# One more stage of lead for the attention scores of a Hymba-style encoder layer, and the ratio of the two softmax sums formed by GpSimd

## The reference, cut to what matters

```python
s = jnp.einsum('bqhcd,bkhcd->bhcqk', qblk, kf) + bias[None, :, None]
pr = jax.nn.softmax(s, axis=-1)
w = pr[:, :, 0] - lam * pr[:, :, 1]
return jnp.einsum('bhqk,bkhe->bqhe', w, vf)
```

## Time and profile before

| | |
|---|---|
| time of the kernel before, median of 3 runs | 1044.28 us (1043.69 to 1045.43) |
| the profiled execution's own time | 1045.79 us |
| its span in the trace | 1044.0 us |
| PE, PEld busy | 1008.5 us (97%), 800.3 us (77%) |
| DVE, ACT, POOL busy | 659.5 (63%), 580.8 (56%), 500.5 us (48%) |
| mean granted TensorE clock | 0.994 of full speed |

### The profile page before, as it was taken

How to read it: one execution, slowest core, us unless ns; L and a number is a source line. 1 busy time by engine, 2 the same in 40 slices (tenths; PEclk the granted TensorE clock), 3 DMA queues, 4 the chain that set the end, 5 groups by cost and what they waited for, 6 DMA issues and landing times.

```text
span 1044.0 us, 15464 instructions
## 1 busy us (share of the span) xinstructions
PE 1008.5 (97%) x5792; PEld 800.3 (77%) x5792; DVE 659.5 (63%) x1055; ACT 580.8 (56%) x890; POOL 500.5 (48%) x404
## 2 busy tenths in 40 slices
PE   8999999999999999989999999999999999999997
PEld 6877777767787888857777777777788888888886
DVE  4654958583493250259999999999966244445423
ACT  7738485744641131269999999999952221122112
POOL 1233245526566550036667767766667244354421
PEclk9999999999999999999999999999999999999999
DMA  9651543323255526839687478363285222432221
GB/s 337 241 169 36 172 147 101 116 81 115 77 162 164 159 81 188 243 101 243 167 197 210 110 192 223 82 159 122 68 300 167 86 87 86 137 121 86 100 87 41
DMA packets 105929, 150.34 MB, mean 144 GB/s; under 512 B 10232, under 2 KB 68728, under 8 KB 105848
## 3 DMA queue, kind: packets, MB, share of 16 engines
q1 hardware_dynamic: 105712, 149.36, 47.5%
q10 hardware_dynamic: 144, 0.00, 0.0%
HBM read 102.07 MB, written 44.11 MB: 140 GB/s over the span
## 4 chain that ended last, share of the span: by engine, by line
PE 63%; DVE 19%; issue 10%; ACT 3%; POOL 2%; DMA 2%; SPq 0%; DVEq 0%; POOLq 0%; ACTq 0%
DVE E_ L1638 11%; PE b_ps L1917 5%; PE b_ps L1919 5%; PE b_ps L1918 5%; PE b_ps L1814 4%; PE g_ps L1816 4%; PE g_ps L1814 4%; PE g_ps L1815 4%; PE b_ps L1815 4%; PE b_ps L1816 4%; PE o_ps L1980 3%; PE w_ps L1963 2%; PE h_ps L1814 2%; PE h_ps L1816 2%; PE h_ps L1815 2%
## 5 line engine op out<-in xcount | busy, mean ns | idle before, releaser
L1251 ACT ACTIVATE E_<-E_,nmax 128x1024 f32<-128x1024 f32 (+1 forms) x184 | 186.7, 1018 | 15.0 <-DVE nmax L1638 14.8
L1638 DVE CUSTOM_DVE_ANT_0 E_<-s_ps,bias 128x1024 f32<-128x1024 f32 (+1 forms) x184 | 188.0, 1056 | 3.6 <-PE s_ps L1930 3.6
L969 POOL TENSOR_TENSOR E_<-E_,ratio 128x576 f32<-128x576 f32 (+3 forms) x92 | 84.5, 919 | 85.8 <-DVE E_ L1654 85.8
L1816 PE MATMUL b_ps<-u_hi,wA_lo 128*128 128x512 f32 x288 | 113.3, 394 | 0.0
L972 POOL TENSOR_TENSOR E_<-E_ 128x576 f32<-128x576 f32 (+3 forms) x92 | 103.7, 1127 | 7.2
L1930 PE MATMUL s_ps<-KL,QL 128*128 128x512 f32 x256 | 90.7, 435 | 13.9 <-DVE nmax L1638 13.1
L1814 PE MATMUL b_ps<-u_hi,wA_hi 128*128 128x512 f32 x240 | 96.7, 403 | 5.0 <-DVE u_lo L1410 2.8
L1815 PE MATMUL b_ps<-u_lo,wA_hi 128*128 128x512 f32 x240 | 94.7, 395 | 0.0
L1963 PE MATMUL w_ps<-ident,E_ 128*128 128x128 f32 x624 | 83.4, 273 | 1.8 <-ACT WT L1282 1.7
L1282 ACT ACTIVATE WT<-w_ps 128x1024 f32<-128x1024 f32 (+1 forms) x96 | 83.3, 868 | 2.8 <-PE w_ps L1963 2.6
L1980 PE MATMUL o_ps<-WT,V 128*64 128x128 f32 x1280 | 84.0, 278 | 0.0
(11 more groups left out here) (228 smaller groups left out, 2329.6 us busy)
## 6 DMA issues: line engine op xcount, KB each, us to landing
QL<-qk_t SPq DMA_DIRECT2D x32, 256.0 KB, 6.9
KL<-qk_t SPq DMA_DIRECT2D x32, 256.0 KB, 8.2
bias<-line_d SPq DMA_DIRECT2D x8, 960.0 KB, 11.8
x_sb<-in_x SPq DMA_DIRECT2D x12, 512.0 KB, 9.0
z_ch<-z_stage SPq DMA_DIRECT2D x24, 256.0 KB, 2.7
qk_t<-qh SPq DMA_DIRECT2D x24, 256.0 KB, 2.3
qk_t<-ql SPq DMA_DIRECT2D x24, 256.0 KB, 2.8
mf<-mix_t SPq DMA_DIRECT2D x24, 256.0 KB, 3.8
```

The costliest lines, as they stand in the source:

```text
L1251: act.activation(e, e, ACT.Exp, bias=nmax[:, n % 5, c:c + 1], scale=-1.0, accum_out=sums[:, n % 5, c:c + 1]).then_inc(e_done, 1)
L1638: dve.tensor_tensor_reduce(weights_at(n)[:, c, 0:n_tok], s_ps[:, c, 0:n_tok], b[:, ::-1], -1.0, 3e38, ALU.add, ALU.min, nmax[:, n % 5, c:c ...
L1816: mm = pe.matmul(dst, sl, mh, start=False, stop=k == n - 1)
```

## The change

The lead of `scores` and `biased` grows from four steps to five (RING), that of `exps` from three to four, that of `combine` from two to three. Seven steps (EARLY), four short and three long ones, have their scores between the V tiles 4 to 10. A long step's second map needs PSUM bank 3, which was a V tile's, so that the V tiles 3, 6 and 9 go to `qT_ps` (`v_bank`); `E_SLOT` only says which slot of the ring a step has. DVE's order in an iteration is now `factor`, `biased(., 0)`, `combine`, `biased(., 1)`. `ratio` is no longer formed on DVE but by `share(n)` on GpSimd, which stands ahead of GpSimd's `combine(n)`. SP's program is the same.

```diff
+        EARLY, RING = 7, 5
+        def steps_to(n, done, lead):
+            return min(NSTEP, max(min(done + n + 1, EARLY + 2), n + 1 + lead)) if n >= 0 else done
+        def due(n, done, lead):
+            return range(steps_to(n - 1, done, lead), steps_to(n, done, lead))
...
+            def share(n):
+                gp.wait_ge(r_done, n + 1)
+                if n >= 4:
+                    gp.wait_ge(w_dve, n - 3)
+                    gp.wait_ge(scaled, n - 3)
+                gp.tensor_scalar(ratio[:, n % 4:n % 4 + 1], sums[:, n % 5, 0:1], rsum[:, n % 24, 1:2], neglam[:],
+                                 ALU.mult, ALU.mult).then_inc(rr_done, 1)
...
             for n in range(NSTEP):
                 blk, head, u, qt = STEPS[n]
+                share(n)
                 combine(n)
...
             def factor(n):
                 dve.wait_ge(e_done, 2 * n + 2)
                 dve.reciprocal(rsum[:, n % 24, :], sums[:, n % 5, :]).then_inc(r_done, 1)
-                dve.wait_ge(r_done, n + 1)
-                if n >= 4:
-                    dve.wait_ge(w_gp, n - 3)
-                dve.scalar_tensor_tensor(out=ratio[:, n % 4:n % 4 + 1], in0=sums[:, n % 5, 0:1],
-                                         scalar=rsum[:, n % 24, 1:2], in1=neglam[:], op0=ALU.mult, op1=ALU.mult
-                                         ).then_inc(rr_done, 1)
...
-                if n + 2 < NSTEP:
-                    factor(n + 2)
-                    combine(n + 2)
-                if n + 4 < NSTEP:
-                    biased(n + 4, 0)
-                    biased(n + 4, 1)
+                for m in due(n, EARLY - 2, RING - 2):
+                    factor(m)
+                for m in due(n, EARLY, RING):
+                    biased(m, 0)
+                for m in due(n, EARLY - 2, RING - 2):
+                    combine(m)
+                for m in due(n, EARLY, RING):
+                    biased(m, 1)
...
-                if 2 * NT + 7 <= n < 2 * NT + 11:
+                if 3 * NT - EARLY - 1 <= n < 3 * NT - 1:
...
-                if n + 4 < NSTEP:
-                    scores(n + 4, 0)
+                for m in due(n, EARLY, RING):
+                    scores(m, 0)
                 turn(n)
-                if n + 4 < NSTEP:
-                    scores(n + 4, 1)
+                for m in due(n, EARLY, RING):
+                    scores(m, 1)
```

More of the change, by code:

```diff
@@ L238, in encoder_layer @@
         phase2.close()
+        E_SLOT = (3, 1, 0, 4, 2)
         def weights_at(n):
-            return Es[:, n, :, :] if n < 4 else E[:, n % 5, :, :]
+            return Es[:, n, :, :] if n < 4 else E[:, E_SLOT[n % 5], :, :]
         def q_tile(u, hh):
@@ L366, in split_at, with v_bank @@
             return {(1, 1): 448, (1, 0): 768, (0, 0): 256, (0, 1): 128}[(int(long_now), int(long_next))]
+        EARLY, RING = 7, 5
[3 more added lines that the diff above has]
+            return range(steps_to(n - 1, done, lead), steps_to(n, done, lead))
+        def v_bank(t):
+            return b_ps[:, t % NB, :] if t % NB or not t else qT_ps[:, 0, :, :].rearrange("p a b -> p (a b)")
         def fill_count(n):
@@ L1264, in _ @@
                     act.wait_ge(x_rs, 3 * NB)
-                act.activation(sq_junk[:, t % 2, :], b_ps[:, t % 3, :], ACT.Copy, scale=rsx[:, t:t + 1]
+                act.activation(sq_junk[:, t % 2, :], v_bank(t), ACT.Copy, scale=rsx[:, t:t + 1]
                                ).then_inc(v_evac, 1)
@@ L1269, in _ @@
                     wl_high(2 * t - 13)
-                if t >= 9:
+                if t >= NT - EARLY:
                     for c in range(2):
-                        exps(t - 9, c)
+                        exps(t - NT + EARLY, c)
             def weights_out(n):
@@ L1305, in _ @@
                 blk, head, u, qt = STEPS[n]
-                if n + 3 < NSTEP:
-                    exps(n + 3, 0)
+                for m in due(n, EARLY, RING - 1):
+                    exps(m, 0)
                 if qt == 1 and blk:
                     heads_out(blk - 1)
-                if n + 3 < NSTEP:
-                    exps(n + 3, 1)
+                for m in due(n, EARLY, RING - 1):
+                    exps(m, 1)
                 if half_out_at(n):
@@ L1673, in wl_low @@
                                   ).then_inc(wl_lo_done, 1)
-            for n in range(4):
+            for n in range(EARLY):
                 for c in range(2):
                     biased(n, c)
-                if n < 2:
-                    wl_low(2 * n)
-                    wl_low(2 * n + 1)
+                if n in (3, 4):
+                    wl_low(2 * n - 6)
+                    wl_low(2 * n - 5)
                 if n >= 2:
@@ L1914, in qkv_tile @@
                     pe.wait_ge(v_evac, 2 + n - 2 * NT - NB + 1)
-                dst = b_ps[:, n % NB, :]
+                if g == 2 and t == NB:
+                    pe.wait_ge(qlo_done, 2 * NT - 1)
+                dst = v_bank(t) if g == 2 else b_ps[:, n % NB, :]
                 for k in range(KC):
@@ L1935, in _ @@
                 qkv_tile(n)
-                if 2 * NT + 7 <= n < 2 * NT + 11:
-                    if n == 2 * NT + 7:
+                if 3 * NT - EARLY - 1 <= n < 3 * NT - 1:
+                    if n == 3 * NT - EARLY - 1:
                         pe.wait_ge(sig_done, UNITS_C * LC)
                     for c in range(2):
-                        scores(n - 2 * NT - 7, c)
+                        scores(n - 3 * NT + EARLY + 1, c)
                 if n == 2:
```

## The result

| | before | after |
|---|---|---|
| median | 1044.69 us (1043.69 to 1045.43, 4 runs) | **1087.2 us** (1084.65 to 1087.94, 4 runs) |
| profiled execution, span | 1044.0 us | 1082.9 us |
| granted clock | 0.994 | 0.989 |
| DVE, ACT, POOL busy | 63%, 56%, 48% | 59%, 54%, 49% |

The ratio is 1.0403, 95% interval 1.0384 to 1.0423: 4% slower. The direction was forecast; the time is 24 us over the forecast's 1063 and outside its range.

What follows compares the result with a forecast made beforehand. DVE was taken as the bound, ACT 5% behind, GpSimd with room. Loop +1.5, `wa_low` +19.2, ACT's lag +1.0, start -0.5 and end -2.6 gave +18.6 on 1045.8: 1064.4, or 1063 for the median; range 1049 to 1072.

Steps and rivals of the forecast that it cites:

- the two `combine`s alternate: Attention loop: DVE's and GpSimd's `combine` can't overlap; long rounds 3.74 us, a head 38.4 against 38.29; forecast case's chance 0.72.
- without its 79 us of waits for DVE: Sign expected in the profile after: GpSimd no longer shows its 79 us of waits for DVE.
- `wa_low` in the round: First two short steps of heads 2 to 5: `wa_low` delays the next `ratio`, 4.8 us a head, 19.2 us together.
- the forecast's wait for `wa_hi`: Sign expected at heads 2 to 5: behind its `wa_low`, GpSimd shows a wait for `wa_hi` of about 2.5 us.
- up to 0.7 at three heads, 0 to 2.1; I take 1: Three heads without `wa_high`: ACT's lag through `half_out` may cost up to 0.7 us each; counted as +1.0 us.
- the short rounds: Loop's short steps, two of each form a head: 2.85 us (768/256), 2.31 (256/256), 2.84 (128/384, DVE's own work).
- ACT's lag and the bias: Loop: ACT's lag through `half_out` counted at 1 us; `biased(12)` waiting for head 1's bias loads at 1.1 us.
- The start: Before the loop: loop starts at 461.3 instead of 458.13, `combine(9)` at 481.9 instead of 483.54, 1.6 us won.
- The end: Behind `combine(95)`: `turn(95)` comes about 3.4 us later instead of 6.0, with PE ahead: -2.6 us.
- The rule weighed: GpSimd contends with DVE instructions having two SBUF inputs, so its halves could shorten; the sum kept their lengths, following a 0.61 us row.

Runs made afterwards that it cites:

- the run with the ratio alone: Kernel before with only `ratio` moved to GpSimd, `share(n)` ahead of its `combine(n)`, leads as before: 1069.24 us (ratio 1.0241).
- lead-four run: Changed kernel with the loop's old leads (scores 4, `exps` 3, `combine` 2), seven early steps, new DVE order and ratio on GpSimd kept: 1067.87 us (1.0232).
- the two with the ratio between: `share(n + 1)` put between GpSimd's multiply and add, `share(0)` ahead of the loop: in the changed kernel 1068.9 us, in the kernel before 1130.1 us.
- the extra operation: Kernel before with one more GpSimd operation of 128x88 behind each add, which nobody waits for: 1047.2 us (1.0029).

## Why the prediction was wrong in size

**Right: the two `combine`s alternate.** Predicted 0.77 + 1.22 + 1.40 + 0.35 = 3.74 us for a long round, measured 3.78; 2.85 predicted for 768 columns, measured 2.89. DVE waits for the ratio where it should, GpSimd's halves kept their 1.15 and 1.43, `share` takes 0.34 to 0.36. That this place of the ratio costs the time is shown by the run with the ratio alone. One of the forecast's signs did not come, and by its own round could not: GpSimd "without its 79 us of waits for DVE". It waits 82.1 us, since in every round its multiply waits for DVE's `combine` (0.80 us in the round shown).

**Right, and dear: `wa_low` in the round.** Predicted 5.75 and 3.6, measured 5.95 and 3.60, with the forecast's wait for `wa_hi` (2.33 us). The price per head is 45.07 - 41.41 = 3.7 instead of 4.8 us, 14.6 instead of 19.2, as the rounds it displaces had grown too. The lead-four run fits the reason given, that ACT comes to `wa_high` an `exps` later: without the fifth step that wait is gone.

**The step that failed: "up to 0.7 at three heads, 0 to 2.1; I take 1", all that was counted for the longer lead inside the loop's other rounds.** The ring has five slots and the lead is five, so `biased(n + 5, 0)` needs `turn(n)` of its own iteration. The forecast asked this question at the start, where it named the wait for a slot, and not in the rounds behind it. There it costs 0.6 us in each of three short rounds of a head (2.95, 3.36 and 3.86 instead of 2.35, 2.72 and 3.21 with lead four), of which the third round gives one back (2.72 instead of 3.37): 1.3 us a head, 9.1 in all. DVE's waits for `w_ps` (27.9 us) and the lead-four run show it.

**A term mis-sized: the short rounds.** The sum took DVE's own 2.84 for the 128-column rounds, and 2.31 for both of 256 columns. With lead four, where no ring wait is left, `combine(73)` to `combine(76)` are 2.72, 3.37 and 3.21 us apart. The kernel before has 2.41, 3.46 and 3.37 at this place: a head of 38.02 us was never the sum of DVE's durations there, since PE's `values` stand ahead of the `scores` that these rounds need. A head without ring waits takes 40.11, predicted 38.4: 1.7 us, 12 in all. Of the 1.7 the short rounds hold 1.35 (11.65 against 10.30); the rest is 0.04 us in each long round. Together 9.1 + 12 - 4.6 (`wa_low`) - 2.1 (ACT's lag and the bias, counted and not seen) = 14.4; the loop was missed by 37.0 - 22.8 = 14.2.

**The start.** From the last transposes on, the first turn comes 3.6 us later than before, near the forecast's 3.2 for the loop's start, and `combine(8)` 74.5 us behind them, where the forecast had 474.4 - 400.4 = 74.0. So far it was right. `combine(9)` was forecast 7.5 us behind `combine(8)` and comes 12.85 us behind it (471.20, 484.05). DVE at the first wait, and two turns on PE:

```profile
476.43 1.22 DVE L1663 CUSTOM_DVE_ANT_0 E_<-s_ps,bias 128x1024 f32<-128x1024 f32 x1 [4.55 <-PE w_ps L1986]
```

```profile
458.56 0.60 PE L1986 MATMUL w_ps<-ident,Es 128*128 128x128 f32 x4
...
463.64 1.08 PE L1986 MATMUL w_ps<-ident,Es 128*128 128x128 f32 x4 [2.85 <-ACT WT L1307]
```

`combine(9)` stands behind `biased(11, 0)`, and that waits for `turn(6)`, which runs at 481.71. The seven turns from 458.56 on come 1.9 to 5.1 us apart; ahead of three of them PE waits for ACT's copies (2.85, 3.17 and 0.78 us). Work done ahead of the loop did not shorten that row of turns.

**The end.** Predicted 2.6 us less, measured 1.3 more: `turn(95)` comes 6.9 us behind `combine(95)` (before 6.0). The last three turns follow each other by 2.27 and 3.52 us, as before, with `values` and half products between them, so PE was not ahead. No run was made for it alone; with lead four this stretch takes 286.6 us instead of 289.1.

**The rule weighed.** GpSimd's multiply and add kept their lengths in the changed kernel, as the sum took it. But beside the multiplies at 602.71 and 607.38 DVE ran `biased`, which reads one tile of SBUF, so these rows did not test a rule on two SBUF inputs. The one at 610.77 does: DVE's ratio lies beside it, and it is the ratio that grows, to 0.30 us, and ends with the multiply. The same rule read for VectorE would have said more. The add of the earlier trace rows runs from 600.13 to 601.56, over the place where DVE forms its ratio:

```profile
601.23 0.35 DVE L1647 SCALAR_TENSOR_TENSOR ratio<-sums,rsum,neglam 128x1 f32<-128x1 f32 x1
```

It takes 0.35 us instead of the 0.22 of the earlier trace rows, and ends with the add, at 601.58. Another sign is a row on record: `combine(95)` takes 1.51 us, where the sum takes 1.08 for 832 columns, and it lies beside an add of GpSimd. These signs stood in the trace and were not followed. They did not alter the sum, since in the changed kernel `combine` starts when GpSimd has just stopped; they do decide what can be done about it.

## What to carry to other kernels

When an operation moves to another engine's queue, write the round as a loop over both queues: if each waits for the other once a step, the period is the sum of both parts and both hand-overs, however much room the busy shares show. When a lead grows, count the slots of the ring: with lead equal to slots, the producer needs the consumer of the same iteration in every step, and not only at the start. And check a sum of durations against the measured distance in the rows of before, in the cheap rounds too; where the two differ, another engine sets the pace.

## What the runs showed of the hardware

**VectorE's scalar_tensor_tensor on SBUF stands still beside GpSimd's adds and multiplies.** Where more than 0.2 us of the GpSimd operation that runs are left when it starts, it ends a fixed time behind that one's end, however much was left:

| columns | alone, us | end behind GpSimd's end, us | rows, in which kernels |
|---|---|---|---|
| 1 | 0.22 | 0.01 to 0.02 | 32, before, behind an add of 576 |
| 128 | 0.35 | 0.15 | 13 and 16, the two with the ratio between |
| 448 | 0.69 | 0.48 to 0.49 | 38 and 47, the same; and 25 with the extra operation |
| 768 | 1.02 | 0.81 to 0.82 | 13 and 14, the same; and 7 with the extra operation |

So 0.2 us of its length can lie beside GpSimd's operation, and nothing is lost where no more than that is left. A start just ahead doesn't help: `combine(95)` of the kernel before starts at 756.26, and this add of GpSimd 0.03 us behind it.

```profile
756.29 0.60 POOL L972 TENSOR_TENSOR E_<-E_ 128x192 f32<-128x192 f32 x1
```

It takes 1.51 instead of 1.08 us and ends 0.88 behind the add. GpSimd can lose as well: in the kernel with the extra operation, one of these starts at 758.72 with 0.92 us of a `combine` to go, and takes 1.12 instead of 0.33 us. Operations that read PSUM and one SBUF tile (`biased` 1.20 to 1.23 us, `heads_scaled` 0.68) and the reciprocal (0.14 to 0.17) kept their lengths beside the same GpSimd operations. The Trainium skill (SBUF — State Buffer, SBUF: two separate sides) describes just this: one port pair for both engines, an exclusive lock held for a whole instruction, which concerns a VectorE operation with two SBUF inputs. The rows agree in the standstill and in what is exempt from it. They do not agree with taking the profile's start for the order of the two: `combine(95)` starts 0.03 us ahead of the add and waits all the same. Hence the kernel before is well placed as it is: GpSimd works while DVE does its two `biased`, and is done when the next `combine` comes.

**TensorE's clock at the start of the loop.** Windows of the changed kernel (us, busy us of each engine, granted clock behind them):

```profile
410.00:450.00 40.00, 39.49 (x174) 32.23 (x174) 16.61 (x36) 17.21 (x31) 7.55 (x12) 1.00 0.69 194
450.00:470.00 20.00, 12.62 (x52) 8.94 (x50) 10.24 (x21) 11.74 (x21) 10.94 (x13) 0.81 0.41 118
470.00:500.00 30.00, 28.82 (x234) 22.77 (x234) 18.48 (x44) 22.30 (x40) 13.66 (x20) 0.90 0.97 221
```

PE was busy 12.6 of 20 us (450 to 470), and four transposes take 1.08 us at 463.64, behind an idle time of 2.85 us, against 0.60 at 458.56: the 1.2 GHz level for part of this stretch. The kernel before, busy 14.9 of the same 20 us, had a granted clock of 1.00 there, and the one with the ratio alone, busy 15.8, had 0.77. So the busy share of the stretch alone does not tell the clock. What it adds to the start was not separated from the waits.
